# Feed-forward gate and up products: 512 columns of rounded and rest tokens at once, the halves added on VectorE

## The chip, the cores and the metric

The kernel runs on one core of a Trainium2 chip. The time is that of one execution on the device in microseconds (us): the median of three runs, 2163.17 us (2163.07 to 2163.5). The profile shown is of a further execution, which took 2163.33 us.

## What is computed

Two hybrid layers follow each other on 256 tokens of width 2048. The change touches the end of the second layer, its feed-forward block, where the weights of gate and up are 2048 x 5632:

```
h2 = rms_norm_2(x, ffn_norm_g)
return x + (jax.nn.silu(h2 @ w_ffn_gate) * (h2 @ w_ffn_up)) @ w_ffn_down
```

All inputs are float32. The kernel gets near float32 products from a reduced format (fp32r) by splitting each operand into a rounded part (hi) and the rest (lo), and adding three products: hi weight by hi token, hi weight by lo token, lo weight by hi token.

## The kernel before

Weights come from memory in units of 1 MB into `raw`, which holds four units; SP issues them. ScalarE rounds half a unit (128 partitions x 1024 numbers, "a half" from here on) into `w_hi` (L832), VectorE subtracts it from `raw` into `w_lo` (L1365). Both have four places, one for each of four consecutive halves; ScalarE may round a half once TensorE has ended the half four before it (semaphore `half_done`), VectorE follows ScalarE (`split_hi`), TensorE follows both (`split_hi`, `split_lo`), and SP refills a unit after `split_lo`. Between the splits each engine does the other work of its stage, in the order in which the code writes it down: nothing is reordered.

Feed-forward gate and up are 11 passes `n`. In each the gate chunk (8 halves) makes 512 gate channels for all 256 tokens, then the up chunk (8 halves) 512 up channels. Weights are the stationary operand, in tiles of 128 x 128; tokens are the moving one, `hf_hi` and `hf_lo`, with 256 columns for each of 16 contraction tiles `k`. The first two contraction tiles of the rests lie apart, in `hf_first`. A half has four contraction tiles and two channel tiles, that is 8 weight tiles; `by_tile` sends 16 products of 256 columns with `w_hi` (hi tokens, lo tokens, in turn), waits for `split_lo`, and sends 8 with `w_lo`. All three kinds add up in the first 256 columns of a PSUM bank; gate uses banks 0, 1, 4, 5 and up 2, 3, 6, 7 (`FF_BANKS`).

VectorE empties the banks. `scale_gate` (after its split of up half 3) multiplies four banks by the token scale `rsb` into `gact`; ScalarE takes the sigmoid after its split of up half 4; `gate_product` (after up half 5) makes two products of 128 x 1024; `up_product` (after half 2 of the next chunk) multiplies four banks with `gact` into `hid`. In the last pass two steps `round_hid` (ScalarE) and `rest_hid` (VectorE) for the down projection come in between. After the last pass the down projection starts: tokens are stationary there (`st_hi`, `st_lo`), weights move with 512 columns, and after its first half TensorE waits for `hid_ready`, which the last `up_product` raises, since the second half overwrites the up banks. ScalarE waits for the same before its split of half 3.

Addresses matter below. `spot_at(x, phase)` places a tile at the next address that is `phase` modulo 256 bytes; PHASE is 64 and FAR is 128. `w_hi`, `w_lo` and `raw` start at 4224 + whole KB, that is at 128 modulo 256; `d0` and `f_at` are 64 modulo 256, and with them `hf_hi`, `hf_lo` and `x1t`; `hf_first`, `st_hi` and `st_lo` are at 128. Every row of these tiles is a whole number of 256 bytes. Those of `h_hi` are 1088 bytes (272 tokens), so that its contraction tiles take all four positions in turn.

Of the kernel before, what the change touches and what calls it, by code (L numbers as in the profile page):

```python
# [15 lines left out]
F32 = mybir.dt.float32  # L16
F32R = mybir.dt.float32r
# [5 lines left out]
P = 128  # L23
D = 2048
T = 256
# [38 lines left out]
def hybrid_layers(nc, a, out):  # L64

    ctx = ExitStack()
    with ctx:
# [68 lines left out]
        f_at = h_at + (PHASE - h_at) % LINE  # L136
        hf_hi = at("hf_hi", [P, KT, T], F32R, f_at)
        hf_lo = at("hf_lo", [P, KT, T], F32R, f_at + 17 * KB)
        hf_first = at("hf_first", [P, 2, T], F32R, spot_at(d0 + 72 * KB, FAR))
        x1t_first = [at(f"x1t_first{k}", [P, T], F32R, spot_at(x, FAR)) for k, x in enumerate((f_at + 32 * KB, rope_at))]  # L140
# [120 lines left out]
        gact = at("gact", [P, 4, T], F32, d0 + 60 * KB)  # L261
        hact = at("hact", [P, 4, T], F32, d0 + 64 * KB)
        dg2 = at("dg2", [P, T], F32, d0 + 68 * KB)
        onesq2 = at("onesq2", [P, P], F32, d0 + 70 * KB)
# [152 lines left out]
        ya_hi_kept = sem("ya_hi_kept")  # L417
        g_sig = sem("g_sig")
        g_kept = sem("g_kept")
        g_prod = sem("g_prod")  # L420
# [139 lines left out]
        def turned_operand(e):  # L560

            def part(w):
                hi, lo = [x1t[:, w // 2, i, 2 * (w % 2):2 * (w % 2) + 2, :] if e in (1, 2)
                          else (hf_hi, hf_lo, mg_hi, mg_lo)[i + 2 * (e == 0)][:, 2 * w:2 * w + 2, :] for i in range(2)]
                rows = [lo[:, x, :] for x in range(2)]
                if w == 0 and e:
                    rows = [x1t_first[x][:, :] if e in (1, 2) else hf_first[:, x, :] for x in range(2)]
                return hi, lo, rows
            return part
# [783 lines left out]
        def _(dve):  # L1353
# [844 lines left out]
            def scale_gate(n):  # L2198
                dve.wait_ge(half_done, 8 * (Q_FFN + 2 * n) + 8)
                for x in range(4):  # L2200
                    ins = dve.tensor_tensor(gact[:, x, :], ps[FF_BANKS[0][x]][:, 0:T], rsb[:, 0:T], ALU.mult)
                ins.then_inc(g_kept, 1)

# [7 lines left out]
            def up_product(n):  # L2211
                dve.wait_ge(half_done, 8 * (Q_FFN + 1 + 2 * n) + 8)
                dve.wait_ge(g_prod, 2 * n + 2)
                for x in range(4):
                    ins = dve.tensor_tensor(hid[:, bass.ds(n * 4 + x, 1), :].rearrange("p k t -> p (k t)"),
                                            ps[FF_BANKS[1][x]][:, 0:T], gact[:, x, :], ALU.mult)
                ins.then_inc(hid_ready, 1)
                dve.wait_ge(hid_ready, n + 1)
# [66 lines left out]
        def _(pe):  # L2285
# [667 lines left out]

            def ht_moving(k):
                return hf_hi[:, k, :], hf_first[:, k, :] if k < 2 else hf_lo[:, k, :]

            def chunk_ff(q, banks, new=None, step=None):

                for h in range(8):
                    if new is not None:  # L2960
                        turned(new, 2 * (2 * (h // 4) + h % 2) + 1)
                    by_tile(q, h, 8 * (h // 4) + 4 * (h % 2), ht_moving,
                            [ps[banks[2 * (h // 2 % 2) + x]][:, 0:T] for x in range(2)], KT - 1)
                    if step is not None:
                        step(h)
# [4 lines left out]
            def ffn(n, first):  # L2970
# [5 lines left out]
                else:  # L2976
                    pe.wait_ge(g_kept, n)
                    chunk_ff(q, FF_BANKS[0])
                if not first:
                    pe.wait_ge(hid_ready, n)  # L2980

# [133 lines left out]
```

## Time and profile before

| | us |
|---|---|
| median of 3 runs | 2163.17 |
| profiled execution | 2163.33 |
| its span, first to last instruction | 2161.5 |
| TensorE busy | 2154.4 (100%) |
| VectorE busy | 1374.5 (64%) |
| ScalarE busy | 1000.6 (46%) |

The span is 1.8 us shorter than the execution. TensorE's two rows are PE, the products, and PEld, the loads of the stationary operand that run beside them. The duration of one product in a row is from its start to its modelled end, and products overlap; so the pace is read from the distance of starts, not from durations. The granted clock is 1.00 in all 40 slices, the higher of its two levels, 2.4 GHz.

### The profile page before, as it was taken

The numbers are of one execution on the slowest core, as the hardware profiler recorded it, in microseconds if no ns is written. First come the engines' busy times: TensorE is split into PE (matmuls) and PEld (weight loads), VectorE is DVE, ScalarE is ACT, GpSimd is POOL, SyncE is SP. The second block draws the span as 40 slices with busy tenths as digits, with TensorE's granted clock in tenths as the row PEclk, the third lists the DMA queues.
The fourth block names the chain that finished last, engine by engine and source line by source line (L and its number), as shares of the span: only waits on it lengthen the run. The fifth ranks groups of instructions, "written<-read, shape, count | busy, mean of one in ns | idle before, by whom it ended". The sixth has DMA issues, their size and how long they took to land.

```text
span 2161.5 us, 34714 instructions
## 1 busy us (share of the span) xinstructions
PE 2154.4 (100%) x14296; PEld 1950.9 (90%) x14296; DVE 1374.5 (64%) x1874; ACT 1000.6 (46%) x1328; POOL 358.2 (17%) x437
## 2 busy tenths in 40 slices
PE   9999999999999999999999999999999999999999
PEld 7898889988888877899999999889999999998887
DVE  6778557968576575776786557455555555554444
ACT  6456644353354444655544445354434444444443
POOL 6563999770000000000000000000000000000000
PEclk9999999999999999999999999999999999999999
DMA  8655655545465644554456565556555555555553
GB/s 278 185 176 171 191 177 169 157 139 175 137 215 198 239 157 156 175 182 150 157 165 202 180 204 190 190 177 195 194 193 194 194 194 188 194 184 197 189 196 134
DMA packets 276530, 396.63 MB, mean 183 GB/s; under 512 B 9399, under 2 KB 198162, under 8 KB 270896
## 3 DMA queue, kind: packets, MB, share of 16 engines
q1 hardware_dynamic: 272704, 384.52, 53.9%
q0 software_dynamic: 3648, 10.37, 1.9%
q8 instruction: 81, 1.33, 0.3%
q14 instruction: 33, 0.27, 0.0%
q10 hardware_dynamic: 64, 0.14, 0.0%
HBM read 392.91 MB, written 2.10 MB: 183 GB/s over the span
## 4 chain that ended last, share of the span: by engine, by line
PE 97%; DVE 1%; ACT 0%; DMA 0%; issue 0%; SPq 0%; DVEq 0%
PE ps L2309 31%; PE ps L2314 16%; PE ps L2299 15%; PE ps L2300 14%; PE ps L2383 11%; PE ps L3000 4%; PE ps L2592 1%; PE ps L2342 0%; PE ps L2539 0%; DMA raw<-w_in 0%; PE ps L2499 0%; DVE w_lo L1365 0%; PE ps L2875 0%; PE ps L2815 0%; PE ps L2835 0%; PE ps L2748 0%
## 5 line engine op out<-in xcount | busy, mean ns | idle before, releaser
L1365 DVE TENSOR_TENSOR w_lo<-raw,w_hi 128x1024 fp32r<-128x1024 f32 x719 | 893.6, 1250 | 602.1 <-ACT w_hi L832 596.8
L832 ACT ACTIVATE w_hi<-raw 128x1024 fp32r<-128x1024 f32 x719 | 752.0, 1058 | 701.3 <-PE ps L2314 420.8
L2309 PE MATMUL ps<-hf_hi,w_hi 128*128 128x256 f32 x1408 | 329.9, 277 | 0.0
L2309 PE MATMUL ps<-hf_lo,w_hi 128*128 128x256 f32 x1232 | 288.1, 276 | 0.0
L2309 PEld LDWEIGHTS ps<-hf_hi,w_hi 128*128 128x128 f32 x1408 | 264.2, 188 | 0.1
L2299 PE MATMUL ps<-w_hi,h_hi 128*128 128x512 f32 x572 | 232.9, 407 | 0.8 <-DVE h_lo L1423 0.8
L2309 PEld LDWEIGHTS ps<-hf_lo,w_hi 128*128 128x128 f32 x1232 | 231.4, 188 | 0.0
L2309 PE MATMUL ps<-x1t,w_hi 128*128 128x256 f32 x1680 | 228.2, 280 | 0.0
L2300 PE MATMUL ps<-w_hi,h_lo 128*128 128x512 f32 x572 | 224.8, 393 | 0.0
L2309 PEld LDWEIGHTS ps<-x1t,w_hi 128*128 128x128 f32 x1680 | 209.3, 188 | 1.4 <-issue 1.0
L2314 PE MATMUL ps<-hf_hi,w_lo 128*128 128x256 f32 x1408 | 188.2, 276 | 0.0
L2314 PEld LDWEIGHTS ps<-hf_hi,w_lo 128*128 128x128 f32 x1408 | 172.7, 188 | 0.0
L2383 PE MATMUL ps<-w_lo,h_hi 128*128 128x512 f32 x572 | 155.3, 393 | 0.0
L2299 PE MATMUL ps<-w_hi,st_hi 128*128 128x512 f32 x348 | 135.5, 389 | 0.0
L2300 PE MATMUL ps<-w_hi,st_lo 128*128 128x512 f32 x348 | 135.4, 389 | 0.0
L2383 PEld LDWEIGHTS ps<-w_lo,h_hi 128*128 128x128 f32 x572 | 107.4, 188 | 24.8
L2299 PEld LDWEIGHTS ps<-w_hi,h_hi 128*128 128x128 f32 x572 | 107.5, 188 | 23.5 <-DVE h_lo L1423 1.1
L2300 PEld LDWEIGHTS ps<-w_hi,h_lo 128*128 128x128 f32 x572 | 107.8, 189 | 21.7
L2314 PE MATMUL ps<-x1t,w_lo 128*128 128x256 f32 x896 | 120.5, 277 | 0.0
L2314 PEld LDWEIGHTS ps<-x1t,w_lo 128*128 128x128 f32 x896 | 110.5, 188 | 0.0
L2309 PE MATMUL ps<-h_hi,w_hi 128*128 128x272 f32 x384 | 100.7, 295 | 0.0
L2309 PE MATMUL ps<-h_lo,w_hi 128*128 128x272 f32 x384 | 98.4, 288 | 0.0
(523 smaller groups left out, 3234.4 us busy)
## 6 DMA issues: line engine op xcount, KB each, us to landing
raw<-w_in SPq DMA_DIRECT2D x163, 1024.0 KB, 5.2
raw<-w_ffn_gate SPq DMA_DIRECT2D x44, 1024.0 KB, 5.1
raw<-w_ffn_up SPq DMA_DIRECT2D x44, 1024.0 KB, 5.1
raw<-w_ffn_down SPq DMA_DIRECT2D x44, 1024.0 KB, 4.9
raw<-w_out SPq DMA_DIRECT2D x32, 1024.0 KB, 5.1
raw<-w_branch SPq DMA_DIRECT2D x16, 1024.0 KB, 5.1
raw<-w_br_hyena SPq DMA_DIRECT2D x8, 1024.0 KB, 5.6
raw<-w_br_attn SPq DMA_DIRECT2D x8, 1024.0 KB, 5.7
```

Of the source, the lines that this page charges most:

```text
L832: act.activation(w_hi[:, h % 4, :, 0:width], raw[:, h // 2, 2 * (h % 2):2 * (h % 2) + 2, 0:width], ACT.Copy).then_inc(split_hi, 1)
L1365: dve.tensor_tensor(w_lo[:, h % 4, :, 0:width], raw[:, h // 2, 2 * (h % 2):2 * (h % 2) + 2, 0:width], w_hi[:, h % 4, :, 0:width].bitcast(F ...
L2299: pe.matmul(dst, left[0], w_h, start=first, stop=False)
L2300: pe.matmul(dst, left[1], w_h, start=False, stop=False)
L2309: pe.matmul(dsts[x], w_h, part, start=(k0 + e == 0 and i == 0), stop=False)
L2314: ins = pe.matmul(dsts[x], w_l, moving(k0 + e)[0], start=False, stop=(k0 + e == last))
L2383: ins = pe.matmul(dst, left(k, i)[0], w_lo[:, h % 4, e, 0:width], start=False, stop=(k == n - 1))
L2592: ins = pe.matmul(ps[6 + c][0:rows, i * (P // 2):(i + 1) * (P // 2)].rearrange("p (k n) -> p k n", n=2 ** (lev - 1)), kl[:, i, c * P:c * P ...
L3000: ins = pe.matmul(ps[bank][:, :], st_hi[:, par, s, cols], w_lo[:, h % 4, e, :], start=False, stop=last)
```

## The change

The tokens' rounded and rest parts are interleaved in one tile `hf` (contraction tile, part, token) at 128 modulo 256, and `hf_first` is gone. `wide_tile` takes the place of `by_tile` in gate and up: for each weight tile one product of 512 columns, `w_hi` by both parts of the tokens, into the whole bank, and one of 256 columns, `w_lo` by the rounded part, added into the bank's second half. It waits for `split_hi` and `split_lo` ahead of the half. VectorE adds the two halves of each bank: four copies from the first halves, four additions of the second halves, and one multiplication of 128 x 1024, each step waiting for the one before (`ff_sum`). The next chunk on the same banks waits for the additions (`ff_sum`) and no longer for `g_kept` or `hid_ready`; the wait for `hid_ready` after the first half of the down projection stays.

```diff
--- before.py
+++ after.py
@@ -134,9 +134,8 @@
         y0 = d0 + 56 * KB
         assert y0 + 34 * KB <= nc.sbuf_usable_end, (y0 + 34 * KB, nc.sbuf_usable_end)
         f_at = h_at + (PHASE - h_at) % LINE
-        hf_hi = at("hf_hi", [P, KT, T], F32R, f_at)
-        hf_lo = at("hf_lo", [P, KT, T], F32R, f_at + 17 * KB)
-        hf_first = at("hf_first", [P, 2, T], F32R, spot_at(d0 + 72 * KB, FAR))
+        hf = at("hf", [P, KT, 2, T], F32R, spot_at(f_at, FAR))
+        hf_hi, hf_lo = (hf[:, :, i, :] for i in range(2))
         x1t_first = [at(f"x1t_first{k}", [P, T], F32R, spot_at(x, FAR)) for k, x in enumerate((f_at + 32 * KB, rope_at))]
         mg_hi = at("mg_hi", [P, KT, T], F32R, spot_at(f_at, FAR))
         mg_lo = at("mg_lo", [P, KT, T], F32R, spot_at(f_at + 16 * KB, FAR))
@@ -260,6 +259,7 @@
         st_lo = at("st_lo", [P, 2, 4, T], F32R, st_at)
         gact = at("gact", [P, 4, T], F32, d0 + 60 * KB)
         hact = at("hact", [P, 4, T], F32, d0 + 64 * KB)
+        up = at("up", [P, 4, T], F32, d0 + 71 * KB)
         dg2 = at("dg2", [P, T], F32, d0 + 68 * KB)
         onesq2 = at("onesq2", [P, P], F32, d0 + 70 * KB)
 
@@ -416,6 +416,7 @@
         ya_lo_kept = sem("ya_lo_kept")
         ya_hi_kept = sem("ya_hi_kept")
         g_sig = sem("g_sig")
+        ff_sum = sem("ff_sum")
         g_kept = sem("g_kept")
         g_prod = sem("g_prod")
         hid_ready = sem("hid_ready")
@@ -563,8 +564,8 @@
                 hi, lo = [x1t[:, w // 2, i, 2 * (w % 2):2 * (w % 2) + 2, :] if e in (1, 2)
                           else (hf_hi, hf_lo, mg_hi, mg_lo)[i + 2 * (e == 0)][:, 2 * w:2 * w + 2, :] for i in range(2)]
                 rows = [lo[:, x, :] for x in range(2)]
-                if w == 0 and e:
-                    rows = [x1t_first[x][:, :] if e in (1, 2) else hf_first[:, x, :] for x in range(2)]
+                if w == 0 and e in (1, 2):
+                    rows = [x1t_first[x][:, :] for x in range(2)]
                 return hi, lo, rows
             return part
 
@@ -2198,8 +2199,15 @@
             def scale_gate(n):
                 dve.wait_ge(half_done, 8 * (Q_FFN + 2 * n) + 8)
                 for x in range(4):
-                    ins = dve.tensor_tensor(gact[:, x, :], ps[FF_BANKS[0][x]][:, 0:T], rsb[:, 0:T], ALU.mult)
-                ins.then_inc(g_kept, 1)
+                    ins = dve.tensor_copy(gact[:, x, :], ps[FF_BANKS[0][x]][:, 0:T])
+                ins.then_inc(ff_sum, 1)
+                dve.wait_ge(ff_sum, 4 * n + 1)
+                for x in range(4):
+                    ins = dve.tensor_tensor(gact[:, x, :], ps[FF_BANKS[0][x]][:, T:W], gact[:, x, :], ALU.add)
+                ins.then_inc(ff_sum, 1)
+                dve.wait_ge(ff_sum, 4 * n + 2)
+                dve.tensor_tensor(gact[:, :, :], gact[:, :, :], rsb[:, 0:T].unsqueeze(1).broadcast_to([P, 4, T]),
+                                  ALU.mult).then_inc(g_kept, 1)
 
             def gate_product(n):
                 dve.wait_ge(g_sig, n + 1)
@@ -2212,9 +2220,14 @@
                 dve.wait_ge(half_done, 8 * (Q_FFN + 1 + 2 * n) + 8)
                 dve.wait_ge(g_prod, 2 * n + 2)
                 for x in range(4):
-                    ins = dve.tensor_tensor(hid[:, bass.ds(n * 4 + x, 1), :].rearrange("p k t -> p (k t)"),
-                                            ps[FF_BANKS[1][x]][:, 0:T], gact[:, x, :], ALU.mult)
-                ins.then_inc(hid_ready, 1)
+                    ins = dve.tensor_copy(up[:, x, :], ps[FF_BANKS[1][x]][:, 0:T])
+                ins.then_inc(ff_sum, 1)
+                dve.wait_ge(ff_sum, 4 * n + 3)
+                for x in range(4):
+                    ins = dve.tensor_tensor(up[:, x, :], ps[FF_BANKS[1][x]][:, T:W], up[:, x, :], ALU.add)
+                ins.then_inc(ff_sum, 1)
+                dve.wait_ge(ff_sum, 4 * n + 4)
+                dve.tensor_tensor(hid[:, bass.ds(n * 4, 4), :], up[:, :, :], gact[:, :, :], ALU.mult).then_inc(hid_ready, 1)
                 dve.wait_ge(hid_ready, n + 1)
 
             def ffn(n, first, second=False, last=False):
@@ -2951,16 +2964,25 @@
             output(Q_OUT2, 4, x1_tile, 2)
 
 
-            def ht_moving(k):
-                return hf_hi[:, k, :], hf_first[:, k, :] if k < 2 else hf_lo[:, k, :]
+            def wide_tile(q, h, k0, banks):
+
+                pe.wait_ge(split_hi, 8 * q + h + 1)
+                pe.wait_ge(split_lo, 8 * q + h + 1)
+                for e in range(4):
+                    for x in range(2):
+                        cols = slice((e % 2) * T + x * P, (e % 2) * T + (x + 1) * P)
+                        pe.matmul(ps[banks[x]][:, :], w_hi[:, h % 4, e // 2, cols],
+                                  hf[:, k0 + e, :, :].rearrange("p s t -> p (s t)"), start=(k0 + e == 0), stop=False)
+                        ins = pe.matmul(ps[banks[x]][:, T:W], w_lo[:, h % 4, e // 2, cols], hf[:, k0 + e, 0, :],
+                                        start=False, stop=(k0 + e == KT - 1))
+                ins.then_inc(half_done, 1)
 
             def chunk_ff(q, banks, new=None, step=None):
 
                 for h in range(8):
                     if new is not None:
                         turned(new, 2 * (2 * (h // 4) + h % 2) + 1)
-                    by_tile(q, h, 8 * (h // 4) + 4 * (h % 2), ht_moving,
-                            [ps[banks[2 * (h // 2 % 2) + x]][:, 0:T] for x in range(2)], KT - 1)
+                    wide_tile(q, h, 8 * (h // 4) + 4 * (h % 2), [banks[2 * (h // 2 % 2) + x] for x in range(2)])
                     if step is not None:
                         step(h)
 
@@ -2974,10 +2996,10 @@
                     pe.wait_ge(x1_ready, 7)
                     chunk_ff(q, FF_BANKS[0], new=3, step=turn_ff)
                 else:
-                    pe.wait_ge(g_kept, n)
+                    pe.wait_ge(ff_sum, 4 * n - 2)
                     chunk_ff(q, FF_BANKS[0])
                 if not first:
-                    pe.wait_ge(hid_ready, n)
+                    pe.wait_ge(ff_sum, 4 * n)
 
                 def row_scale(h):
                     if h == 0:
```

On TensorE, a half of the feed-forward (rows that name tiles: `ps` is PSUM) is before, from the start of a half on:

```order
L2309 MATMUL ps<-hf_hi,w_hi 128x256 [waits split_hi]
L2309 MATMUL ps<-hf_lo,w_hi 128x256
L2309 MATMUL ps<-hf_hi,w_hi 128x256
L2309 MATMUL ps<-hf_lo,w_hi 128x256
...
L2314 MATMUL ps<-hf_hi,w_lo 128x256 [waits split_lo]
L2314 MATMUL ps<-hf_hi,w_lo 128x256 x7
```

and after:

```order
L2974 MATMUL ps<-hf,w_hi 128x512 [waits split_lo,split_hi]
L2976 MATMUL ps<-hf,w_lo 128x256
L2974 MATMUL ps<-hf,w_hi 128x512
L2976 MATMUL ps<-hf,w_lo 128x256
L2974 MATMUL ps<-hf,w_hi 128x512
L2976 MATMUL ps<-hf,w_lo 128x256
```

24 products of 256 columns became 8 of 512 and 8 of 256: the sum of the columns is the same.

On VectorE, the last pass and the step into the down projection (`gact` and `up` hold gate and up channels, `hid` their product, `st_lo` the rests for the down projection) stand before as

```order
L2201 TENSOR_TENSOR gact<-ps,rsb 128x256 [waits half_done]
L2201 TENSOR_TENSOR gact<-ps,rsb 128x256 x3
L1365 TENSOR_TENSOR w_lo<-raw,w_hi 128x1024 [waits split_hi] x2
L2206 TENSOR_TENSOR gact<-gact,hact 128x1024 [waits g_sig]
L2208 TENSOR_TENSOR gact<-gact,rsb 128x1024 [waits g_prod]
L2250 TENSOR_TENSOR st_lo<-hid,st_hi 128x1024 [waits hs_hi]
L1365 TENSOR_TENSOR w_lo<-raw,w_hi 128x1024 [waits split_hi]
...
L2215 TENSOR_TENSOR hid<-ps,gact 128x256 [waits g_prod,half_done]
L2215 TENSOR_TENSOR hid<-ps,gact 128x256 x3
L1365 TENSOR_TENSOR w_lo<-raw,w_hi 128x1024 [waits split_hi,hid_ready]
```

and after as

```order
L2202 COPY gact<-ps 128x256 [waits half_done]
L2202 COPY gact<-ps 128x256 x3
L2206 TENSOR_TENSOR gact<-ps,gact 128x256 [waits ff_sum]
L2206 TENSOR_TENSOR gact<-ps,gact 128x256 x3
L2209 TENSOR_TENSOR gact<-gact,rsb 128x1024 [waits ff_sum]
L1366 TENSOR_TENSOR w_lo<-raw,w_hi 128x1024 [waits split_hi] x2
...
L2223 COPY up<-ps 128x256 [waits g_prod,half_done]
L2223 COPY up<-ps 128x256 x3
L2227 TENSOR_TENSOR up<-ps,up 128x256 [waits ff_sum]
L2227 TENSOR_TENSOR up<-ps,up 128x256 x3
L2230 TENSOR_TENSOR hid<-up,gact 128x1024 [waits ff_sum]
L1366 TENSOR_TENSOR w_lo<-raw,w_hi 128x1024 [waits split_hi,hid_ready]
```

Each emptying of the banks grew from four instructions to nine, in the same place between the splits.

## Rows read from the trace of the kernel before

**Rows 1.** The page: busy time of the engines, and the chain that ended last.
```profile
PE 2154.4 (100%) x14296; PEld 1950.9 (90%) x14296; DVE 1374.5 (64%) x1874; ACT 1000.6 (46%) x1328; POOL 358.2 (17%) x437
PE 97%; DVE 1%; ACT 0%; DMA 0%; issue 0%; SPq 0%; DVEq 0%
```

**Rows 2.** Stage view, feed-forward: us, busy (count) by engine, granted clock, DMA share, GB/s.
```profile
1480.00:1524.00 44.00, 44.00 (x389) 44.00 (x388) 24.94 (x27) 17.94 (x17) 0.00 (x0) 1.00 0.60 193
```

**Rows 3.** Tile view of `hf_hi`: count, duration ns, first and last start.
```profile
L2309 PE MATMUL ps<-hf_hi,w_hi x1408: 276/276/468, 1436.3 to 1917.0; 128*128 128x256 f32 x176
L2314 PE MATMUL ps<-hf_hi,w_lo x1408: 276/276/281, 1438.1 to 1918.0; 128*128 128x256 f32 x176
```

**Rows 4.** Timeline of PE, one half: start us, duration, line, tiles, count.
```profile
1500.48 0.28 PE L2309 MATMUL ps<-hf_hi,w_hi 128*128 128x256 f32 x1
...
1503.20 0.28 PE L2309 MATMUL ps<-hf_hi,w_hi 128*128 128x256 f32 x1
```

**Rows 5.** Timeline of PE, the next half, with `hf_first`.
```profile
1503.31 0.28 PE L2309 MATMUL ps<-hf_first,w_hi 128*128 128x256 f32 x1
...
1504.14 0.28 PE L2309 MATMUL ps<-hf_hi,w_hi 128*128 128x256 f32 x1
...
1505.96 0.28 PE L2309 MATMUL ps<-hf_hi,w_hi 128*128 128x256 f32 x1
```

**Rows 6.** Timeline of PE, down projection, three halves of 12 products.
```profile
2002.62 0.39 PE L2299 MATMUL ps<-w_hi,st_hi 128*128 128x512 f32 x1
...
2010.79 0.39 PE L2299 MATMUL ps<-w_hi,st_hi 128*128 128x512 f32 x1
```

**Rows 7.** Timeline of PE, 512 columns with other stationary tiles: `x1t`, `h_hi`.
```profile
1430.76 0.39 PE L2299 MATMUL ps<-w_hi,x1t 128*128 128x512 f32 x1
...
1433.51 0.39 PE L2299 MATMUL ps<-w_hi,x1t 128*128 128x512 f32 x1
...
702.22 0.39 PE L2299 MATMUL ps<-w_hi,h_hi 128*128 128x512 f32 x1
...
710.51 0.39 PE L2299 MATMUL ps<-w_hi,h_hi 128*128 128x512 f32 x1
```

**Rows 8.** VectorE's groups, feed-forward from 1480 to 1910: busy us, mean ns.
```profile
L1365 DVE TENSOR_TENSOR w_lo<-raw,w_hi 128x1024 fp32r<-128x1024 f32 x157 | 192.3, 1225 | 181.2 <-ACT w_hi L832 180.1
L2215 DVE TENSOR_TENSOR hid<-ps,gact 128x256 f32 (+1 forms) x40 | 14.2, 416 | 5.6 <-PE ps L2314 5.6
L2201 DVE TENSOR_TENSOR gact<-ps,rsb 128x256 f32<-128x256 f32 x40 | 14.1, 414 | 0.0
L2208 DVE TENSOR_TENSOR gact<-gact,rsb 128x1024 f32<-128x1024 f32 x10 | 12.3, 1225 | 0.3
```

**Rows 9.** VectorE's groups, 1440 to 1480: one copy out of PSUM.
```profile
L2239 DVE COPY rsb<-ps 128x256 f32<-128x256 f32 x1 | 0.4, 425 | 0.9 <-PE ps L2985 0.9
```

**Rows 10.** Timeline: the split of the half that starts at 1508.64.
```profile
1500.68 1.06 ACT L832 ACTIVATE w_hi<-raw 128x1024 fp32r<-128x1024 f32 x1 [1.66 <-PE ps L2314]
...
1501.77 1.22 DVE L1365 TENSOR_TENSOR w_lo<-raw,w_hi 128x1024 fp32r<-128x1024 f32 x1 [1.49 <-ACT w_hi L832]
```

**Rows 11.** Timelines of VectorE and PE in the last pass.
```profile
1898.75 1.41 DVE L2201 TENSOR_TENSOR gact<-ps,rsb 128x256 f32<-128x256 f32 x4
...
1907.95 1.22 DVE L1365 TENSOR_TENSOR w_lo<-raw,w_hi 128x1024 fp32r<-128x1024 f32 x1
...
1911.81 1.07 PE L2314 MATMUL ps<-hf_hi,w_lo 128*128 128x256 f32 x8
```

**Rows 12.** Timeline: step from the feed-forward into the down projection.
```profile
1918.16 0.27 PE L2295 MATMUL ps<-ident 128*128 128x128 f32 x1
...
1918.36 1.42 DVE L2215 TENSOR_TENSOR hid<-ps,gact 128x256 f32<-128x256 f32 x4 [0.34 <-PE ps L2314]
...
1919.81 1.06 ACT L832 ACTIVATE w_hi<-raw 128x1024 fp32r<-128x1024 f32 x1 [3.05 <-DVE hid L2215]
...
1921.03 0.39 PE L2299 MATMUL ps<-w_hi,st_hi 128*128 128x512 f32 x1
```

## The prediction

> **What bounds the kernel now.** I read the page first: TensorE is busy for the whole span, and it holds 97% of the chain that ended last [rows 1]. So only what changes TensorE's own time, or makes it wait, can move the end. The stage view says the same of the feed-forward: in 44 us TensorE is busy for 44, VectorE for 25, ScalarE for 18, the DMAs for 0.60 of theirs, and the granted clock is 1.00, the higher level of 2.4 GHz [rows 2]. The tile view gives the stage's ends: the first product starts at 1436.3, the down projection at 1918.16 [rows 3, 12], so gate and up last 481.9 us. They have 22 chunks of 8 halves with 8 weight tiles each: 1408 tiles, 3 products each (1408 with `w_hi` by `hf_hi`, 1408 with `w_lo` [rows 3], and as many by the rests).
>
> The question is what sets TensorE's pace: the columns or the number of instructions. The timeline answers it. A half of 24 products of 256 columns takes from 1500.48 to 1503.20, that is 2.72 us, 113.3 ns for each [rows 4]. In the down projection 36 products of 512 columns take from 2002.62 to 2010.79, that is 8.17 us, 226.9 ns for each [rows 6]. Twice the columns take twice the time (2 x 113.3 = 226.6), although every product of either size has its own load of the stationary operand. A fixed part for each instruction doesn't show; the loads are hidden in both.
>
> **The change part by part.**
>
> TensorE's products: for a weight tile 3 x 113.3 = 340 ns goes, and 226.9 + 113.3 = 340 ns comes. 1408 loads and 1408 instructions fewer are worth nothing as long as the columns set the pace. Term: 0.
>
> The Trainium skill, page "TensorE: Matmul & The Clock Gate", section "Back-to-back issue gap", gives a start-to-start time of columns / 2.4 plus about 2.5 ns. By it 256 columns would take 109.2 ns and 512 would take 215.8, and 1408 products fewer would save 1408 x 2.5 ns = 3.5 us. The trace differs: 113.3 and 226.9, with nothing fixed between them, so I keep 0.
>
> The rests of the first two contraction tiles: halves 0 and 2 of each chunk read them from `hf_first`. Such a half takes from 1503.20 to 1505.96, 2.76 us instead of 2.72; its first 8 products, hi and first in turn, take 0.94 us, 117.5 ns each [rows 4, 5]. There are 2 x 22 = 44 such halves: 44 x 0.04 = 1.8 us. `hf_first` is at 128 modulo 256 and `hf_hi` at 64. With the change all tokens lie at 128, as `w_hi` and `w_lo` do. Is this place slow in itself, or only the turning between the two? In the down projection the moving weights and the stationary tokens are both at 128, and the pace there is the clean one [rows 6]. With the stationary `x1t` at 64 it is 2.75 us for 12, 229.2 ns, and with the rows of `h_hi`, at all four positions, 8.29 us for 36, 230.3 ns [rows 7]. So equal positions are the good case for 512 columns, and I take them to be good for 256 too. Term: -1.8 us. The bounds are -1.8 (clean) and, if all 256-column products keep 117.5, -1.8 + 1408 x 4.2 ns = +4.1 us; if the 512-column ones lose 3.4 ns as well (230.3 against 226.9), another 4.8, +8.9.
>
> The Trainium skill, same page, section "Part 2: What happens when you issue a matmul", says that the moving operand and the weight load have SBUF read ports of their own and don't take bandwidth from each other. By it the place of a tile would cost nothing and the term would be safe. No run here shows the ports; the row of `hf_first` shows that something about a tile's place costs 4.2 ns, so the upper bound stays.
>
> The wait ahead of a half: TensorE now needs `w_lo` when a half starts, not 16 products later. ScalarE's split at 1500.68, released by the half that ended at 1500.48, is for the half that starts three halves later, at 1500.48 + 3 x 2.72 = 1508.64; `w_lo` is ready at 1501.77 + 1.22 = 1502.99 [rows 10]. That is 5.6 us early. Term: 0.
>
> VectorE's emptying: before, 4 products out of PSUM at 14.1 / 40 = 0.35 us, 1.4 us for a chunk [rows 8]. After, 4 copies, 4 additions, one product of 128 x 1024 at 1.23 and two waits on its own engine. The copy out of PSUM shows once, alone, at 425 ns, against 414 for the product [rows 8, 9], so I take 0.35 for both in a row: 1.4 + 1.4 + 1.2 + 2 x 0.03 = 4.1 us (0.3 us of idle time for 10 waits [rows 8]); with 0.425 for the copies 4.4. Each of the 22 emptyings is 2.7 us longer. Behind it stand on VectorE the next split, on ScalarE the sigmoid with the next split, and SP's refill of `raw`. In most passes 2.7 us is taken from a lead of 5.6 us and is gone again some halves later, since VectorE needs only 1.2 of every 2.7 us for a split. The cover is thinnest in the last pass, where `round_hid` and `rest_hid` stand in between: `w_lo` of up half 6 ends at 1907.95 + 1.22 = 1909.17 and the half starts at 1911.81 + 8 x 0.113 = 1912.72, a lead of 3.55 us [rows 11]. The chain to it (emptying from 1898.75, sigmoid, rounding, split, product, rests) is serial, so it all moves by 2.7, and 0.85 us is left. Term: 0; without that cover, what is missing counts once. The next chunk's wait for `ff_sum` concerns additions that end a whole chunk (22 us) earlier.
>
> The step into the down projection: here the emptying is on the path. It starts at 1918.36 and ended after 1.42 us, before TensorE had finished the first down half at 1921.03 [rows 12]. Now `hid_ready` comes at 1918.36 + 4.1 = 1922.5, and TensorE waits from 1921.03, about 1.5 us, once. ScalarE's split of half 3 waits for it too (1919.81 becomes 1922.5), is ready with `w_lo` near 1924.9, and is needed at 1922.5 + 2 x 2.72 = 1928. Term: +1.5 us (0 to +1.9).
>
> Sum: 0 - 1.8 + 0 + 0 + 1.5 = -0.3 us. The profiled execution took 2163.33, its span 2161.5; so 2163.0 for that execution, and since it lies 0.16 above the median of the runs, 2162.9.
>
> **The rivals.**
>
> 1. The place of the tokens costs (slower). `hf` at 128 gives its products the pace of `hf_first`. For it: 117.5 ns is the only pace in these rows of 256 columns moving from 128. Against it: rows 6, with 128 on both sides, are clean; and in rows 5 hi products at 64 are as slow as their neighbours, so the turning may be the cause. Price: 5.9 us on top of the forecast, 2168.8; if the 512-column products pay too (4.8, or 11.8 at 2 x 4.2 ns) 2173.6 to 2180.6. It decides from about 3.3 ns a pair on (4.6 us over 1408 pairs).
>
> 2. Fewer instructions pay (faster). At 2.4 GHz 256 columns would need 106.7 ns; if all of the 6.6 ns above that belonged to the instruction, 1408 fewer would save 9.3 us: 2153.6. Against it: 512 columns then would take 213.3 + 6.6 = 219.9 ns, and rows 6 show 226.9. By the page's 2.5 ns the time would be 2159.4.
>
> 3. VectorE's cover fails. If PSUM operations took 0.7 instead of 0.35 us, an emptying would be 5.5 us longer than before instead of 2.7; the last pass would miss by 5.5 - 3.55 = 2 us and the down step would wait 2.8 more: 2167.7, and up to 2172 if other passes miss by half a us each. For it: copies next to each other aren't in the trace. Against it: the alone copy's 425 ns.
>
> 4. The down step's wait doesn't show, because the copies are quicker: 2161.4, the same verdict as the forecast.
>
> **How the numbers follow.** What a measurement of this kernel can tell from no change is 0.2%, 4.3 us: 2158.9 to 2167.5. Forecast with rival 4: 74%, by itself 2161 to 2166. Rival 1: 16%, nearly all of it slower. Rival 2: 5%, of which a part stays inside 0.2%. Rival 3: 5%. So faster 4%, same 76%, slower 20%. The range takes in rival 1's first step and rival 2's small price: 2160 to 2171.
>
> **What would show it.** In the profile after: a half of the feed-forward takes 2.72 us, also halves 0 and 2 (2.76 or more: rival 1; 2.67: rival 2); the distance from a 512-column start to the next is 340 ns; VectorE's nine instructions take about 4.1 us; no idle time of TensorE ends with `w_lo` in the passes; one wait of about 1.5 us ends with `hid` after the first down half. A feed-forward stage of other than 480 us, or a gap at each pass, would make the prediction wrong.

## The result, and the profile after

The changed kernel takes 2172.64 us (median of 6 runs, 2172.4 to 2172.99) against 2163.28 (6 runs of before, 2163.07 to 2163.5): a ratio of 1.0043, interval 1.0032 to 1.0054, 9.4 us slower. I had forecast 2162.9 and no change. The profiled execution took 2172.42 us, its span is 2170.6, and the granted clock is 1.00 throughout, the 2.4 GHz level, as before; the clock has no part in it.

The page's engine row and chain row after (to be read against [rows 1]):

```profile
PE 2162.3 (100%) x12888; PEld 1900.4 (88%) x12888; DVE 1428.5 (66%) x1984; ACT 999.3 (46%) x1328; POOL 358.1 (16%) x437
PE 97%; DVE 1%; ACT 0%; DMA 0%; issue 0%; SPq 0%; DVEq 0%
```

TensorE has 1408 products and loads fewer and yet is busy longer. The tile view of `hf` (count, duration, first and last start) gives the feed-forward, as [rows 3] did before:

```profile
L2974 PE MATMUL ps<-hf,w_hi x1408: 389/391/580, 1436.2 to 1925.3; 128*128 128x512 f32 x176
L2976 PE MATMUL ps<-hf,w_lo x1408: 274/280/282, 1436.5 to 1925.6; 128*128 128x256 f32 x176
```

The stage starts at the same moment and ends at 1925.67 (below), not at 1918.16: 489.4 us instead of 481.9. The timeline of one half, start in the first column, answers to [rows 4]:

```profile
1503.09 0.39 PE L2974 MATMUL ps<-hf,w_hi 128*128 128x512 f32 x1
1503.32 0.28 PE L2976 MATMUL ps<-hf,w_lo 128*128 128x256 f32 x1
1503.43 0.39 PE L2974 MATMUL ps<-hf,w_hi 128*128 128x512 f32 x1
...
1505.86 0.39 PE L2974 MATMUL ps<-hf,w_hi 128*128 128x512 f32 x1
```

A pair is one product of 512 columns and the one of 256 behind it. From 1503.09 to 1505.86 eight pairs take 2.77 us, 347 ns each, where 340 were expected: as a mean over the half, 230.0 ns from a 512-column start to the next start, 116.7 after a 256-column one. It is so in every half without a stall, also in those that had read `hf_first`: 176 x (2.773 - 2.720) = 9.3 us more, less the 1.8 us of `hf_first`, is the stage's 7.5.

VectorE's groups, from 1480 to 1910 (busy, mean; then idle time before and what ended it), answer to [rows 8]:

```profile
L2223 DVE COPY up<-ps 128x256 f32<-128x256 f32 x40 | 14.2, 416 | 5.2 <-PE ps L2976 5.2
L2227 DVE TENSOR_TENSOR up<-ps,up 128x256 f32<-128x256 f32 x40 | 14.2, 415 | 0.3
L2209 DVE TENSOR_TENSOR gact<-gact,rsb 128x1024 f32<-128x1024 f32 x10 | 12.2, 1225 | 0.3
```

A copy costs what an addition costs, 14.2 / 40 = 0.355 us in a row, and a wait of VectorE for itself 0.3 / 10 = 0.03: an emptying is 1.42 + 1.42 + 1.22 + 0.06 = 4.1 us. In the last pass, where the cover was thinnest, the timeline has the split of up half 6 and TensorE's start of it:

```profile
1917.73 1.22 DVE L1366 TENSOR_TENSOR w_lo<-raw,w_hi 128x1024 fp32r<-128x1024 f32 x1
...
1920.12 0.39 PE L2974 MATMUL ps<-hf,w_hi 128*128 128x512 f32 x1
```

`w_lo` ends at 1917.73 + 1.22 = 1918.95, 1.2 us early (0.85 was expected, 3.55 it had been [rows 11]); no wait for it shows. The step into the down projection answers to [rows 12]:

```profile
1925.67 0.27 PE L2308 MATMUL ps<-ident 128*128 128x128 f32 x1
...
1925.87 1.42 DVE L2223 COPY up<-ps 128x256 f32<-128x256 f32 x4 [0.40 <-PE ps L2976]
...
1927.32 1.41 DVE L2227 TENSOR_TENSOR up<-ps,up 128x256 f32<-128x256 f32 x4
...
1928.77 1.22 DVE L2230 TENSOR_TENSOR hid<-up,gact 128x1024 f32<-128x1024 f32 x1
1930.03 2.01 ACT L833 ACTIVATE w_hi<-raw 128x1024 fp32r<-128x1024 f32 x2 [5.81 <-DVE hid L2230]
1930.05 0.50 PE L2312 MATMUL ps<-w_hi,st_hi 128*128 128x512 f32 x1 [1.36 <-DVE hid L2230]
```

From the stage's end to the second down half it is 1930.05 - 1925.67 = 4.38 us, and it was 2.87 before: the new wait of 1.5 us. Together 7.5 + 1.5 = 9.0 of the 9.1 us between the two profiled executions.

### The profile page after: what moved, and what is told of

Its sections match the earlier page's. It is cut to its first block, busy times and chain, and to the rows that moved or that the text cites. A ratio compares the mean times of both kernels' runs of the same rounds, so it can differ in the third digit from the quotient of the medians.

```text
span 2170.6 us, 32184 instructions
## 1 busy us (share of the span) xinstructions
PE 2162.3 (100%) x12888; PEld 1900.4 (88%) x12888; DVE 1428.5 (66%) x1984; ACT 999.3 (46%) x1328; POOL 358.1 (16%) x437
## 4 chain that ended last, share of the span: by engine, by line
PE 97%; DVE 1%; ACT 0%; DMA 0%; issue 0%; SPq 0%; DVEq 0%
PE ps L2322 16%; PE ps L2974 15%; PE ps L2312 14%; PE ps L2313 14%; PE ps L2396 11%; PE ps L2327 8%; PE ps L2976 8%; PE ps L3022 4%; PE ps L2605 1%; PE ps L2355 0%; PE ps L2552 0%; DMA raw<-w_in 0%; PE ps L2512 0%; DVE w_lo L1366 0%; PE ps L2888 0%; PE ps L2828 0%
## 5 line engine op out<-in xcount | busy, mean ns | idle before, releaser
L2974 PE MATMUL ps<-hf,w_hi 128*128 128x512 f32 x1408 | 488.5, 391 | 0.0
L2976 PE MATMUL ps<-hf,w_lo 128*128 128x256 f32 x1408 | 394.1, 280 | 0.0
L2974 PEld LDWEIGHTS ps<-hf,w_hi 128*128 128x128 f32 x1408 | 263.3, 187 | 57.8
L2976 PEld LDWEIGHTS ps<-hf,w_lo 128*128 128x128 f32 x1408 | 266.0, 189 | 0.1
L3022 PE MATMUL ps<-w_lo,st_hi 128*128 128x512 f32 x348 | 93.0, 389 | 0.0
L2312 PE MATMUL ps<-w_hi,x1t 128*128 128x512 f32 x224 | 88.7, 396 | 0.0
```

The source lines that it names most:

```text
L2312: pe.matmul(dst, left[0], w_h, start=first, stop=False)
L2974: pe.matmul(ps[banks[x]][:, :], w_hi[:, h % 4, e // 2, cols], hf[:, k0 + e, :, :].rearrange("p s t -> p (s t)"), start=(k0 + e == 0), stop ...
L2976: ins = pe.matmul(ps[banks[x]][:, T:W], w_lo[:, h % 4, e // 2, cols], hf[:, k0 + e, 0, :], start=False, stop=(k0 + e == KT - 1))
L3022: ins = pe.matmul(ps[bank][:, :], st_hi[:, par, s, cols], w_lo[:, h % 4, e, :], start=False, stop=last)
```

## The experiments

The wait at the step into the down projection was as forecast. What had to be found is why products of the same number of columns in sum run 2% slower. Theory A was my rival 1, the place of the tokens against the weights (a place is the start of a tile modulo 256 bytes); theory B, that turning between two kinds of product costs something at each. The weights stay at 128 in all runs. Times below are medians, the ratio is to the kernel before with its 95% interval.

**Tokens at 64.** One edit to the changed kernel:

```diff
-        hf = at("hf", [P, KT, 2, T], F32R, spot_at(f_at, FAR))
+        hf = at("hf", [P, KT, 2, T], F32R, f_at)
```

> The changed kernel with one edit: the tile hf starts at 64 modulo 256 instead of 128. Theory A (the place of the tokens against the weights costs): a pair of 512 + 256 columns goes from 346.7 ns back to 340.0, a half from 2.77 to 2.72 us, the time from 2172.6 to about 2163.2. Theory B (turning between products of 512 and 256 columns, or between w_hi and w_lo, costs 3.4 ns at each product whatever the place): pair 346.7, half 2.77, time 2172.6.

Measured: 2181.9 us, 1.0085 (1.0069 to 1.0102). Neither: it got slower by another 9 us. The tile view:

```profile
L2974 PE MATMUL ps<-hf,w_hi x1408: 389/397/586, 1436.5 to 1934.9; 128*128 128x512 f32 x176
```

(1934.9 - 1436.5) / 1407 = 354.2 ns a pair, small stalls of the first pass included, where the changed kernel has 347.6 by the same working (353.3 and 346.7 in halves without a stall). The place matters, but 128 is not the bad one.

**Grouped.** The changed kernel, sizes in two groups within a half:

```diff
                         pe.matmul(ps[banks[x]][:, :], w_hi[:, h % 4, e // 2, cols],
                                   hf[:, k0 + e, :, :].rearrange("p s t -> p (s t)"), start=(k0 + e == 0), stop=False)
+                for e in range(4):
+                    for x in range(2):
+                        cols = slice((e % 2) * T + x * P, (e % 2) * T + (x + 1) * P)
                         ins = pe.matmul(ps[banks[x]][:, T:W], w_lo[:, h % 4, e // 2, cols], hf[:, k0 + e, 0, :],
                                         start=False, stop=(k0 + e == KT - 1))
```

> The changed kernel with one edit: a half sends its 8 products of 512 columns first and then its 8 of 256, tokens still at 128. Theory A (place): nothing changes, half 2.77 us, time about 2172.6. Theory B (turning between the two kinds of product): only 2 of 16 products have a neighbour of the other kind, so the extra 0.054 us of a half falls to under 0.01, half 2.72 us, time about 2163.5.

Measured: 2175.92 us, 1.0058 (1.0041 to 1.0075). Timeline of one half (start, duration of the whole group):

```profile
1599.87 2.00 PE L2974 MATMUL ps<-hf,w_hi 128*128 128x512 f32 x8
1601.71 1.12 PE L2979 MATMUL ps<-hf,w_lo 128*128 128x256 f32 x8
1602.66 2.00 PE L2974 MATMUL ps<-hf,w_hi 128*128 128x512 f32 x8
```

The 512-column group takes 1.84 us, 230 ns each, and its single starts show the first five at 228 to 236 and the last three at 226.7 on the mean: it settles. The 256-column group takes 0.95 us, 119 ns each, 120 after its second product. Grouping does not help, so B as stated falls: products of 256 columns from 128 are slow among their own kind.

**Before, with all tokens at 128.**

```diff
-        hf_hi = at("hf_hi", [P, KT, T], F32R, f_at)
-        hf_lo = at("hf_lo", [P, KT, T], F32R, f_at + 17 * KB)
+        hf_hi = at("hf_hi", [P, KT, T], F32R, spot_at(f_at, FAR))
+        hf_lo = at("hf_lo", [P, KT, T], F32R, spot_at(f_at + 17 * KB, FAR))
```

> The kernel before with one edit: hf_hi and hf_lo start at 128 modulo 256 (hf_first is there already), so that all tokens lie where the changed kernel has them; products of 256 columns in the order of before. Theory A: every product costs 116.7 to 117.5 ns instead of 113.3, a half 2.80 to 2.82 us instead of 2.72, the time 2176 to 2180. Theory B: the pace stays 113.3, and the halves with hf_first lose their extra 0.04 us: time about 2161.5.

Measured: 2189.55 us, 1.0121 (1.0104 to 1.0138):

```profile
L2309 PE MATMUL ps<-hf_hi,w_hi x1408: 277/283/468, 1436.2 to 1943.1; 128*128 128x256 f32 x176
```

506.9 us over 1407 tiles is 360.3 ns, 120.1 for a product: worse than A's 117.5. As A said, 256 columns from 128 against weights at 128 are slow. But the first run spoke against A, and the next one did so much more.

**Before, with `hf_first` at 64.**

```diff
-        hf_first = at("hf_first", [P, 2, T], F32R, spot_at(d0 + 72 * KB, FAR))
+        hf_first = at("hf_first", [P, 2, T], F32R, d0 + 72 * KB)
```

> The kernel before with one edit: hf_first moves from 128 to 64 modulo 256, where hf_hi and hf_lo are. Both theories: its 44 halves go from 2.76 to 2.72 us, the time from 2163.2 to about 2161.5 (Theory A: because of the place; Theory B: because the turning between two places is gone). If neither holds and the distance between the tiles counts, the halves stay at 2.76.

Measured: 2179.3 us, 1.0074 (1.0057 to 1.0091). Taking away the slow products cost 16 us. The timeline shows where it begins:

```profile
1458.91 0.28 PE L2309 MATMUL ps<-hf_hi,w_hi 128*128 128x256 f32 x1
...
1461.63 0.59 PE L2985 MATMUL ps<-dg,onesq 128*128 128x256 f32 x2
1461.87 0.47 PE L2309 MATMUL ps<-hf_hi,w_hi 128*128 128x256 f32 x1
...
1464.88 0.28 PE L2309 MATMUL ps<-hf_hi,w_hi 128*128 128x256 f32 x1
...
1467.71 0.28 PE L2309 MATMUL ps<-hf_hi,w_hi 128*128 128x256 f32 x1
```

The first up half takes 2.72 us (1458.91 to 1461.63). Then comes the row-scale step, two products `ps<-dg,onesq` and a pause, once in the feed-forward, and from the half after it on every half takes 2.83 (1464.88 to 1467.71), to the end of the stage: 117.8 ns a product, with the same tiles at the same places that ran at 113.3 just before. So a pace lasts: something throws TensorE from one to the other, and it stays there. Not every interruption does: eight products with `ident` at 1441.7 in the same run are followed, after a few slower starts, by 113.3 again. That is theory C: the kernel before is thrown too, and its `hf_first`, at 128 where the other tokens are at 64, whose 0.04 us a half I had booked as a loss, is what brings it back. Theory D is that such a tile only helps nearby.

**One kick.** A kick is here a few reads of a tile at another place, meant to throw the pace. The kernel before with its rests of contraction tiles 0 and 1 at 64, and a copy at 128 that is read in one chunk alone, the up chunk of the first pass, in halves 0 and 2:

```diff
+        hf_rest = at("hf_rest", [P, 2, T], F32R, d0 + 72 * KB)
...
-                return hf_hi[:, k, :], hf_first[:, k, :] if k < 2 else hf_lo[:, k, :]
+                return hf_hi[:, k, :], hf_rest[:, k, :] if k < 2 else hf_lo[:, k, :]
+            def ht_kick(k):
+                return hf_hi[:, k, :], hf_first[:, k, :] if k < 2 else hf_lo[:, k, :]
...
-                chunk_ff(q + 1, FF_BANKS[1], step=row_scale if first else None)
+                chunk_ff(q + 1, FF_BANKS[1], step=row_scale if first else None, moving=ht_kick if first else ht_moving)
```

> The kernel before with the rests of contraction tiles 0 and 1 at 64 modulo 256 like all other tokens (as in the run that put hf_first there and took 2179.3 us), and a second copy of them at 128 that only the up chunk of the first pass reads. Theory C (the pace is a state that lasts: TensorE's reads of weights and of tokens stay in one of two relations until something disturbs it; the row-scale product in the first up chunk throws it into the slow one, 117.6 ns, and a token tile at 128 brings it back to 113.3): one use is enough, halves after the first up chunk take 2.72 us in all ten passes, time about 2161.6. Theory D (a tile at 128 helps only near where it is read; without it the pace is 117.6): halves go back to 2.83 us from the second pass on, time about 2178.

Measured: 2161.64 us (11 runs, 2161.36 to 2162.21) against 2163.28 (15 runs, 2162.97 to 2164.16), 0.9992 (0.9983 to 1.0001). C holds, to 0.04 us (the slow pace in the trace is 117.8 ns, not 117.6). The timeline around the kick, and a half far from it:

```profile
1462.52 0.28 PE L2312 MATMUL ps<-hf_lo,w_hi 128*128 128x256 f32 x1
...
1464.29 1.11 PE L2317 MATMUL ps<-hf_hi,w_lo 128*128 128x256 f32 x8
1465.23 0.28 PE L2312 MATMUL ps<-hf_hi,w_hi 128*128 128x256 f32 x1
1465.35 0.28 PE L2312 MATMUL ps<-hf_first,w_hi 128*128 128x256 f32 x1
...
1467.09 1.07 PE L2317 MATMUL ps<-hf_hi,w_lo 128*128 128x256 f32 x8
1467.99 0.28 PE L2312 MATMUL ps<-hf_hi,w_hi 128*128 128x256 f32 x1
...
1601.27 0.28 PE L2312 MATMUL ps<-hf_hi,w_hi 128*128 128x256 f32 x1
...
1603.99 0.28 PE L2312 MATMUL ps<-hf_hi,w_hi 128*128 128x256 f32 x1
```

The half behind the row-scale step runs at the slow pace: eight products take 0.94 us (1464.29 to 1465.23). Half 2 then reads `hf_first` four times, from 1465.35 on, and at its end eight products take 0.90 (1467.09 to 1467.99). 133 us later a half still takes 2.72. The four reads in half 0 came ahead of the row-scale step, so four are enough. This version is also the fastest of all; none of its 11 runs overlaps with the 15 of before, though the interval of the ratio just reaches 1.

**A kick for the new order.** The changed kernel at 64, contraction tiles 2 and 3 as three products of 256 with their rests at 128:

```diff
+                        if k0 + e in (2, 3):
+                            pe.matmul(ps[banks[x]][:, 0:T], w_hi[:, h % 4, e // 2, cols], hf[:, k0 + e, 0, :],
+                                      start=False, stop=False)
+                            pe.matmul(ps[banks[x]][:, T:W], w_hi[:, h % 4, e // 2, cols], hf_kick[:, k0 + e - 2, :],
+                                      start=False, stop=False)
+                        else:
...
```

> The changed kernel with hf at 64 modulo 256, and contraction tiles 2 and 3 sent as three products of 256 columns with their rests from a tile at 128. Theory C: if the 512 + 256 order at 64 has a fast state, the halves that don't read the tile at 128 take 2.72 us, and the time is about 2164 to 2165; if it has none, they go on at 2.83 us and the time is about 2181. Theory D: 2.83 us there, time 2180 to 2182.

Measured: 2180.97 us, 1.0081 (1.0066 to 1.0097). The last eight of the twelve pairs between two kicks:

```profile
1599.80 0.40 PE L2983 MATMUL ps<-hf,w_hi 128*128 128x512 f32 x1
...
1602.63 0.28 PE L2978 MATMUL ps<-hf,w_hi 128*128 128x256 f32 x1
```

2.83 us. The first two pairs behind a kick take 347 and 345 ns, then it is 353 again: this kick does not bring the pairs of 512 and 256 to the pace of 340.2 ns that I had summed.

**The other two places.** `FAR` in the line of `hf` replaced by 192 and by 0.

> The changed kernel with hf at 192 modulo 256. Known: 2.77 us a half at 128, 2.83 at 64. Theory C: the order of products gives a cycle whose length depends on the place; one of the four places may be free of conflicts (2.72 us, time about 2163), and nothing says which: 2163 to 2190. If the place alone set the pace as I thought at first, 128 would be the best of the four and this is slower than 2172.6.

> The changed kernel with hf at 0 modulo 256; theories and bounds as for 192: 2163 (a half 2.72 us) to 2190.

Measured: 2181.85 us (1.0086, 1.0071 to 1.0102) and 2178.81 (1.0072, 1.0056 to 1.0087); the tile view at 192:

```profile
L2974 PE MATMUL ps<-hf,w_hi x1408: 392/397/579, 1436.2 to 1934.7; 128*128 128x512 f32 x176
```

and at 0:

```profile
L2974 PE MATMUL ps<-hf,w_hi x1408: 387/396/582, 1436.3 to 1931.6; 128*128 128x512 f32 x176
```

354.3 and 352.0 ns a pair. With 347.6 at 128 and 354.2 at 64, the changed kernel had the best of four places, and none reaches 340.2.

**Grouped, at 64.**

> The changed kernel, a half's 8 products of 512 columns first and then the 8 of 256, and hf at 64 modulo 256. With hf at 128 the grouped order gave 226.7 ns at the end of the 512-column group and 120 in the 256-column group (2175.9 us). Theory C1 (in groups of one size each place has its own lasting states; 256 columns from 64 have a fast one): the 256-column products run at 113.3, and what remains is how fast 512 columns from 64 are: 2163 if clean, up to 2173 if they stay at 233. Theory C2 (any change of size within a half throws the state out): slow in both groups, about 2180.

Measured: 2172.51 us, 1.0042 (1.0025 to 1.0059).

```profile
1601.51 2.02 PE L2974 MATMUL ps<-hf,w_hi 128*128 128x512 f32 x8
1603.37 1.07 PE L2979 MATMUL ps<-hf,w_lo 128*128 128x256 f32 x8
1604.29 2.02 PE L2974 MATMUL ps<-hf,w_hi 128*128 128x512 f32 x8
```

The mirror image of the first grouped run: the 256-column group settles at 113.3 (0.92 us in all, its first product 118), and the 512-column one does not settle, 1.86 us, 233 ns each. In groups, with weights at 128, 512 columns settle at their quick pace from 128 and 256 columns at theirs from 64. C2 falls.

**By turns, equal sizes.** The kernel before, its three products of 256 columns for each weight tile in a row:

```diff
...
+                        pe.matmul(dsts[x], w_hi[:, h % 4, e // 2, cols], hi, start=(k0 + e == 0), stop=False)
+                        pe.matmul(dsts[x], w_hi[:, h % 4, e // 2, cols], lo, start=False, stop=False)
+                        ins = pe.matmul(dsts[x], w_lo[:, h % 4, e // 2, cols], hi, start=False, stop=(k0 + e == KT - 1))
...
```

> The kernel before with another order of its products of 256 columns in gate and up: for each weight tile w_hi by hi tokens, w_hi by lo tokens, w_lo by hi tokens; places as before (64, hf_first at 128); the wait for split_lo ahead of the half. Theory S (products of different sizes next to each other prevent the fast state): all sizes are equal here, so 113.3 ns and 2.72 us for a half, time about 2163. Theory W (turning between w_hi and w_lo at every product prevents it): a half takes 2.77 us or more, time 2172 or more.

Measured: 2165.61 us, 1.001 (1.0 to 1.002). 24 products in the first gate chunk, the row-scale step, and 24 products in a later pass:

```profile
1447.90 0.28 PE L2965 MATMUL ps<-hf_hi,w_hi 128*128 128x256 f32 x1
...
1450.72 0.28 PE L2965 MATMUL ps<-hf_hi,w_hi 128*128 128x256 f32 x1
...
1462.03 0.28 PE L2965 MATMUL ps<-hf_hi,w_hi 128*128 128x256 f32 x1
...
1463.09 0.28 PE L2965 MATMUL ps<-hf_hi,w_hi 128*128 128x256 f32 x1
...
1463.44 0.59 PE L2998 MATMUL ps<-dg,onesq 128*128 128x256 f32 x2
...
1464.92 0.28 PE L2965 MATMUL ps<-hf_hi,w_hi 128*128 128x256 f32 x1
...
1466.62 0.28 PE L2965 MATMUL ps<-hf_hi,w_hi 128*128 128x256 f32 x1
...
1600.26 0.28 PE L2965 MATMUL ps<-hf_hi,w_hi 128*128 128x256 f32 x1
...
1602.98 0.28 PE L2965 MATMUL ps<-hf_hi,w_hi 128*128 128x256 f32 x1
```

2.82 us first, 2.72 later: both paces in one run, the quick one from the first up chunk to the end. W falls: turning between `w_hi` and `w_lo` at every product leaves the quick pace possible. But what switches is not what switched in the kernel before. Three halves had read `hf_first` by 1462.03, and nine products still took 1.06 us from there to 1463.09, 117.8 ns each; behind the row-scale step 15 take 1.70 us (1464.92 to 1466.62), 113.3 each. Here the same step throws TensorE to the quick pace, and the reads at 128 ahead of it did not. What is left of the 2.2 us against before (2163.37 in its runs) is the slower first chunk and costlier halves with `hf_first` (2.80 us instead of 2.76).

**Two places.** What was still open is whether mixed sizes fail because at one place one of them is always at its bad one (P), or because of the mixing (S). The changed kernel, rounded tokens of contraction tiles 0 to 7 for the 256-column products from a second copy at 64:

```diff
-                                        w_lo[:, h % 4, e // 2, cols], hf[:, k0 + e, 0, :],
+                                        w_lo[:, h % 4, e // 2, cols],
+                                        hf_two[:, k0 + e, :] if k0 + e < KT // 2 else hf[:, k0 + e, 0, :],
```

> The changed kernel, in which the 256-column products of contraction tiles 0 to 7 (halves 0 to 3 of each chunk) read the rounded tokens from a second copy at 64 modulo 256, while the 512-column ones read theirs at 128 as before; halves 4 to 7 as they are (gact and hact lie elsewhere to make room). Theory P (each size has its own good place: in groups, 512 columns ran at 226.7 ns from 128 and 256 columns at 113.3 from 64, while 256 from 128 took 120; the pair of 346.7 is 226.7 + 120): halves 0 to 3 fall to 2.72 us, halves 4 to 7 stay at 2.77, time about 2172.6 - 88 x 0.054 = 2168. Theory S (two sizes in turn have no fast state wherever the tokens lie): halves 0 to 3 stay at 2.77 us or get slower, time 2172.6 or more.

Measured: 2178.89 us, 1.0072 (1.0055 to 1.0088). Halves 0 to 3 take 2.80, not 2.72: P falls, as far as the two sizes are sent in turn. And halves 4 to 7, whose products and token places are those of the changed kernel but for the halves ahead of them, have two paces (timeline: one half in the first gate chunk, one much later):

```profile
1451.10 0.39 PE L2978 MATMUL ps<-hf,w_hi 128*128 128x512 f32 x1
...
1453.87 0.39 PE L2978 MATMUL ps<-hf,w_hi 128*128 128x512 f32 x1
...
1678.98 0.40 PE L2978 MATMUL ps<-hf,w_hi 128*128 128x512 f32 x1
...
1681.81 0.40 PE L2978 MATMUL ps<-hf,w_hi 128*128 128x512 f32 x1
```

2.77 and 2.83 us: mixed sizes have two paces too, but the better one seen is 2.77. The two sizes in groups and at their two places together, 512 columns from 128 and then 256 from 64, were not run.

**VectorE's part alone.** Two runs for the terms that held. The old emptying, for gate and in the same way for up:

```diff
-                    ins = dve.tensor_copy(gact[:, x, :], ps[FF_BANKS[0][x]][:, 0:T])
...
-                    ins = dve.tensor_tensor(gact[:, x, :], ps[FF_BANKS[0][x]][:, T:W], gact[:, x, :], ALU.add)
...
+                    ins = dve.tensor_tensor(gact[:, x, :], ps[FF_BANKS[0][x]][:, 0:T], rsb[:, 0:T], ALU.mult)
```

> The changed kernel with the emptying of the banks as before (four products each, from the first halves; the sums of w_hi by lo tokens and w_lo by hi tokens in the second halves are left out). My prediction's terms: VectorE's added work costs only the wait at the step into the down projection, 1.5 us: 2171.1, and a feed-forward half stays at 2.77 us. Rival: VectorE's added reads of PSUM or its later splits slow TensorE: a half goes back towards 2.72 us, time about 2162 to 2165.

Measured: 2171.11 us, 1.0036 (1.0022 to 1.005): 1.5 us less, as the terms said. The feed-forward kept its 2.77 us a half (tile view):

```profile
L2962 PE MATMUL ps<-hf,w_hi x1408: 389/391/580, 1437.0 to 1926.1; 128*128 128x512 f32 x176
```

And the wait moved to the additions:

```diff
-                        pe.wait_ge(hid_ready, D_FF // W)
+                        pe.wait_ge(ff_sum, 4 * (D_FF // W))
```

> The changed kernel with one edit: after the first half of the down projection TensorE waits for the last additions (ff_sum) and not for hid_ready. The product of 128 x 1024 (1.2 us) leaves the path, so the wait of 1.5 us there falls to about 0.25: 2172.6 becomes about 2171.3. If the wait is covered by something else, 2172.6.

Measured: 2171.27 us, 1.0036 (1.0022 to 1.005), 1.4 less. The row that answers to 1930.05 above, and the last products before it:

```profile
1927.99 1.07 PE L3022 MATMUL ps<-w_lo,st_hi 128*128 128x512 f32 x4
...
1929.16 0.50 PE L2312 MATMUL ps<-w_hi,st_hi 128*128 128x512 f32 x1
```

It was due at 1927.99 + 4 x 0.227 = 1928.90 and starts at 1929.16: a wait of 0.26.

## Why the prediction was wrong, by its own steps

**TensorE's products, term 0: wrong, +9.3 us.** "Twice the columns take twice the time" is true of the rows I took, which are the quick paces of two other arrangements. It is also true of the paces to which the grouped runs settle, 226.7 ns for 512 columns from 128 and 113.3 for 256 from 64. I carried both paces over to an order that exists nowhere in the kernel before, 512 and 256 in turn, and summed 226.9 + 113.3 = 340.2. That order settled at 346.7 at best, at all places tried. A fixed part for each instruction still doesn't show in the settled paces, and rival 2 did not come in; what failed is the step that a product's pace belongs to its shape.

**The rests of the first two contraction tiles, term -1.8 us: right in size, wrong in meaning.** The 0.04 us of 44 halves do go when they alone are taken away in the right manner (one kick: -1.6 us). Taken away altogether, in the kernel before, this costs 16 us, since there they bring the quick pace back after the row-scale step. I saw that hi products at 64 next to them are slow too and thought of turning; I did not ask what the pace would be without them. "Equal positions are the good case for 512 columns, and I take them to be good for 256 too" is the sentence that the third run refutes most plainly: 120.1 ns.

**Rival 1** foresaw the side, and its first two prices, 4.2 and 4.2 + 3.4 = 7.6 ns a pair, bracket the measured 6.7 (I let the range end between them, at 2171); but its mechanism, a bad place at 128, does not explain it alone. For it: in the grouped run 256 columns from 128 settled at 120, and 226.7 + 120 is 346.7. Against it: 64, 0 and 192 are worse, reading half of the 256-column tokens from 64 made it worse too, and the starts show the excess at both sizes, 230.0 and 116.7. **Rival 3** and **rival 4** did not occur.

**Wait ahead of a half, VectorE's emptying, the step into the down projection: right.** 4.1 us for an emptying, 1.2 us left in the last pass against 0.85 forecast, a wait of 1.5 us; the last two runs take it away by 1.5 and 1.4 us.

The Trainium skill's section "Part 2: What happens when you issue a matmul" in "TensorE: Matmul & The Clock Gate" says that the weight load takes no bandwidth from the moving operand. What I drew from it in the prediction, that by it the place of a tile would cost nothing, does not agree with these runs: one edit of a tile's address by 64 bytes moved the time by 16 us. Whether the load and the tokens share anything no run shows. The 2.5 ns a product of the section "Back-to-back issue gap" on the same page of the Trainium skill would have saved 3.5 us, by estimate; no run shows them.

What stays open is the cause behind the paces. The runs show that the place of the tokens, the sizes, their order and what ran before together decide the pace; they don't show whether it is the weight load and the token stream that meet, as theory C has it, and the place of the weights was never moved. Nor was the place in PSUM: in every run of the new order both sizes write the second half of the same bank. That 512 and 256 in turn do not reach 340.2 ns a pair is shown for the arrangements run here only.

## What to carry to other kernels

Where TensorE is the bound, compare the distance of starts in steady stretches with the best seen for that shape: a pace of 2 to 4% above it can be one of two that a stretch falls into (117.8 against 113.3 ns, 2.83 against 2.77 us), and a single different step can start or end it, in either direction. Before taking a slow-looking access away, look at the pace behind it, and before the change at what else throws the pace; a forecast for a new order of sizes needs a range up to the slowest pace seen for each shape. And an addition that frees a bank should release it itself, not the product behind it.

## What the runs showed of the hardware that I had not expected

- The same products of 256 columns (tokens at 64, weights at 128 modulo 256) run at 113.3 or 117.8 ns, each for hundreds of us, at a granted clock of 1.00. In the order of the kernel before, the row-scale step and its pause switch to the slow pace and four reads of a tile at 128 to the quick one; with the products by turns the same step switches to the quick one.
- With tokens and weights both at 128, products of 512 columns settle at 226.7 ns after five, and those of 256 columns at 120.
- 512 and 256 columns in turn take 346.7 ns a pair at 128 and about 351 to 353 at 0, 64 and 192 in halves without a stall; behind halves with two places up to 354 at 128 as well.
- VectorE's copy of 128 x 256 out of PSUM costs what an addition with an SBUF operand does, 0.355 us in a row.
